# Attention products of the sample tokens with the values, issued between the dense matmuls of the next unit

## The reference

```python
D_MODEL, SEQ, DEC_SEQ, PAST_LEN = 2048, 256, 64, 256
N_HEADS, HEAD_DIM = 16, 128

h = _rms_norm(x, g_mix)
z = h @ w_in                      # GLU a, b | q | k | v | indexer | gates
...
s = jnp.einsum('qhd,qkhd->qhk', q, kg) * HEAD_DIM ** -0.5
s = jnp.where(valid[:, None, :], s, -jnp.inf)
p = jax.nn.softmax(s, axis=-1)
o = jnp.einsum('qhk,qkhd->qhd', p.astype(v.dtype), vg)
...
m = jax.nn.sigmoid(ga) * c + jax.nn.sigmoid(gb) * (o @ w_attn_out)
x = x + m @ w_out
h = _rms_norm(x, g_ffn)
x = x + (jax.nn.silu(h @ w_gate) * (h @ w_up)) @ w_down
```

## Time and profile before

| | us |
|---|---|
| median of 3 runs | 2058.59 |
| lowest and highest run | 2056.78, 2058.63 |
| span of the profiled execution | 2055.5 |

### The profile page before, as it was taken

How to read it: one execution, slowest core, us unless ns; L and a number is a source line. 1 busy time by engine, 2 the same in 40 slices (tenths; PEclk the granted TensorE clock), 3 DMA queues, 4 the chain that set the end, 5 groups by cost and what they waited for, 6 DMA issues and landing times.

```text
span 2055.5 us, 37840 instructions
## 1 busy us (share of the span) xinstructions
PE 2036.4 (99%) x13897; PEld 2018.5 (98%) x13897; DVE 1116.9 (54%) x1658; ACT 810.4 (39%) x1133; POOL 44.6 (2%) x55
## 2 busy tenths in 40 slices
PE   9999999999999999999999999999999999999997
PEld 8999999999999999999999999999999999999997
DVE  6865777778876343344546444445444333344454
ACT  5633344444446333333334333333333232333343
POOL 2200000000020000000000000000000000000000
PEclk9999999999999999999999999999999999999999
DMA  7445566666655545444445454454454454454443
GB/s 199 123 144 155 154 165 163 155 168 161 164 138 159 155 150 153 143 143 143 143 153 162 140 159 149 137 163 147 139 163 148 139 162 144 143 155 141 143 133 112
DMA packets 362094, 308.84 MB, mean 150 GB/s; under 512 B 74271, under 2 KB 359543, under 8 KB 362048
## 3 DMA queue, kind: packets, MB, share of 16 engines
q1 hardware_dynamic: 360832, 305.32, 50.4%
q0 software_dynamic: 1184, 2.90, 0.5%
q10 hardware_dynamic: 32, 0.01, 0.0%
HBM read 299.98 MB, written 8.19 MB: 150 GB/s over the span
## 4 chain that ended last, share of the span: by engine, by line
PE 97%; DMA 1%; DVE 1%; SPq 0%; ACT 0%; issue 0%; DVEq 0%
PE M L589 26%; PE M L591 26%; PE M L590 26%; PE T L590 5%; PE T L591 5%; PE T L589 5%; DMA x_tok<-in_x_prompt 1%; PE T L768 0%; PE S L746 0%; DVE c_all L1660 0%; DMA v_tok<-out_v_s 0%; PE S L744 0%; PE S L899 0%; PE S L745 0%; PE S L657 0%; PE T L772 0%
## 5 line engine op out<-in xcount | busy, mean ns | idle before, releaser
L1303 DVE TENSOR_TENSOR w_lo<-w_raw,w_hi 128x1024 fp32r<-128x1024 f32 (+1 forms) x556 | 669.2, 1219 | 544.7 <-ACT w_hi L942 531.9
L942 ACT ACTIVATE w_hi<-w_raw 128x1024 fp32r<-128x1024 f32 (+1 forms) x556 | 574.4, 1051 | 581.6 <-PE M L591 398.6
L589 PE MATMUL M<-h_hi,w_hi 128*128 128x320 f32 x1792 | 560.0, 312 | 0.9 <-DVE w_lo L1303 0.9
L591 PE MATMUL M<-h_hi,w_lo 128*128 128x320 f32 x1792 | 553.7, 309 | 0.0
L590 PE MATMUL M<-h_lo,w_hi 128*128 128x320 f32 x1792 | 553.6, 309 | 0.0
L589 PE MATMUL M<-o_hi,w_hi 128*128 128x320 f32 x1664 | 513.5, 309 | 0.0
L591 PE MATMUL M<-o_hi,w_lo 128*128 128x320 f32 x1664 | 513.1, 308 | 0.0
L590 PE MATMUL M<-o_lo,w_hi 128*128 128x320 f32 x1664 | 513.1, 308 | 0.0
L589 PEld LDWEIGHTS M<-h_hi,w_hi 128*128 128x128 f32 x1792 | 336.5, 188 | 3.0 <-issue 2.4
L590 PEld LDWEIGHTS M<-h_lo,w_hi 128*128 128x128 f32 x1792 | 336.5, 188 | 0.5
L591 PEld LDWEIGHTS M<-h_hi,w_lo 128*128 128x128 f32 x1792 | 336.3, 188 | 0.0
(11 more groups left out here) (303 smaller groups left out, 1267.9 us busy)
## 6 DMA issues: line engine op xcount, KB each, us to landing
w_raw<-in_w_in SPq DMA_DIRECT2D x208, 512.0 KB, 3.9
w_raw<-in_w_gate SPq DMA_DIRECT2D x88, 512.0 KB, 4.5
w_raw<-in_w_up SPq DMA_DIRECT2D x88, 512.0 KB, 4.4
w_raw<-in_w_down SPq DMA_DIRECT2D x88, 512.0 KB, 3.4
w_raw<-in_w_attn_out SPq DMA_DIRECT2D x32, 512.0 KB, 5.1
w_raw<-in_w_out SPq DMA_DIRECT2D x32, 512.0 KB, 3.5
w_raw<-in_w_conv_out SPq DMA_DIRECT2D x16, 512.0 KB, 3.5
x_tok<-in_x_prompt SPq DMA_DIRECT2D x4, 512.0 KB, 9.0
```

The source lines that it names most:

```text
L589: mm(out, w_hi[:, s, wc:wc + m], x_hi, start=start, stop=False)
L591: done = mm(out, w_lo[:, s, wc:wc + m], x_hi, start=False, stop=stop)
L942: act_fn(w_hi[:, s, 0:n], w_raw[:, s, 0:n], ACT.Copy).then_inc(hi_ready, 1)
L1303: v.tensor_tensor(w_lo[:, s, 0:n], w_raw[:, s, 0:n], w_hi[:, s, 0:n].bitcast(f32), ALU.subtract)\
```

## The change

`attend` issues only the two prompt products of an out step. The three sample products become a list of three calls, `sample_out(h)`. The next unit gets them as `between` and issues one of them behind each of its first three slices of block 0, that is behind its 3rd, 6th and 9th dense matmul. pv_done is still signalled by the third. In W_HEAD out 0 goes into unit 7 and out 1 into unit 9; for the last pair out 0 goes into unit 6 of the first merge iteration and out 1 into unit 8. The waits stay where they were, ahead of the prompt products. No other engine's program changes.

```diff
+            BETWEEN_AT = ((0, 0), (0, 1), (0, 2))
+
+            def unit(ph, i, u, k0, first, last, banks, hi, lo, n=NU, free=None, part=None, between=()):
...
                         done = mm(out, w_lo[:, s, wc:wc + m], x_hi, start=False, stop=stop)
+                        if (b, kk) in BETWEEN_AT[:len(between)]:
+                            between[BETWEEN_AT.index((b, kk))]()
...
                     mm(out[:, P:TP], v_tok[:, 1, hc], pT[:, TP:PP], start=False, stop=True)
-                    mm(out[:, TP:T], cv_tok[:, 0, hc], pT_past[:, h * TS:(h + 1) * TS], start=True, stop=False)
-                    mm(out[:, TP:T], cv_tok[:, 1, hc], pT_past[:, P + h * TS:P + (h + 1) * TS], start=False, stop=False)
-                    mm(out[:, TP:T], v_tok[:, 2, hc], pT[:, PP + h * TS:PP + (h + 1) * TS], start=False, stop=True)\
-                        .then_inc(pv_done, 1)
+
+            def sample_out(h):
+
+                hc = slice(h * P, (h + 1) * P)
+                out = T0[:, 3 * TS + TP:3 * TS + T]
+                return (lambda: mm(out, cv_tok[:, 0, hc], pT_past[:, h * TS:(h + 1) * TS], start=True, stop=False),
+                        lambda: mm(out, cv_tok[:, 1, hc], pT_past[:, P + h * TS:P + (h + 1) * TS],
+                                   start=False, stop=False),
+                        lambda: mm(out, v_tok[:, 2, hc], pT[:, PP + h * TS:PP + (h + 1) * TS],
+                                   start=False, stop=True).then_inc(pv_done, 1))
+
+            def between_of(step):
+                return sample_out(int(step[-1])) if step in ("out 0", "out 1") else ()
...
+                def inside(u):
+                    return between_of(HEAD_STEPS[u - 1]) if 1 <= u <= len(HEAD_STEPS) else ()
+                head_units(i, extra, inside)
...
+            def last_pair_inside(u):
+                return between_of(HEAD_STEPS[u]) if 6 <= u < 9 else ()
+
+            merge_units(0, last_pair_and_norm, last_pair_inside)
```

More of the change, by code:

```diff
@@ L568, in _ @@
             TILES = ((2, T - P), (0, 0), (1, P))
-            def unit(ph, i, u, k0, first, last, banks, hi, lo, n=NU, free=None, part=None):
+            BETWEEN_AT = ((0, 0), (0, 1), (0, 2))
+            def unit(ph, i, u, k0, first, last, banks, hi, lo, n=NU, free=None, part=None, between=()):
                 s = u % 4
@@ L769, in attend, with head_units @@
                     mm(out[:, P:TP], v_tok[:, 1, hc], pT[:, TP:PP], start=False, stop=True)
-                    mm(out[:, TP:T], cv_tok[:, 0, hc], pT_past[:, h * TS:(h + 1) * TS], start=True, stop=False)
-                    mm(out[:, TP:T], cv_tok[:, 1, hc], pT_past[:, P + h * TS:P + (h + 1) * TS], start=False, stop=False)
-                    mm(out[:, TP:T], v_tok[:, 2, hc], pT[:, PP + h * TS:PP + (h + 1) * TS], start=False, stop=True)\
-                        .then_inc(pv_done, 1)
+            def sample_out(h):
[8 more added lines that the diff above has]
+                return sample_out(int(step[-1])) if step in ("out 0", "out 1") else ()
             pe.sem_inc(pv_done, 1)
-            def head_units(i, extra):
+            def head_units(i, extra, inside=None):
                 for u in range(12):
@@ L786, in head_units @@
                         free = (act_evac, lambda b: at(ACT_EV, W_HEAD, i, b + 1))
-                    unit(W_HEAD, i, u, KU * (u % 4), u % 4 == 0, u % 4 == 3, SET[g % 2], h_hi, h_lo, free=free)
+                    unit(W_HEAD, i, u, KU * (u % 4), u % 4 == 0, u % 4 == 3, SET[g % 2], h_hi, h_lo, free=free,
+                         between=() if inside is None else inside(u))
                     extra(u)
@@ L813, in extra, with merge_units @@
                         attend(i - 1, HEAD_STEPS[u])
-                head_units(i, extra)
-            def merge_units(i, extra=None):
+                def inside(u):
+                    return between_of(HEAD_STEPS[u - 1]) if 1 <= u <= len(HEAD_STEPS) else ()
+                head_units(i, extra, inside)
+            def merge_units(i, extra=None, inside=None):
                 for u in range(14):
@@ L832, in merge_units @@
                     last = u in (3, 7, 11, 13)
-                    unit(W_MERGE, i, u, KU * (u % 4), u % 4 == 0, last, SET[g % 2], hi, lo, free=free, part=part)
+                    unit(W_MERGE, i, u, KU * (u % 4), u % 4 == 0, last, SET[g % 2], hi, lo, free=free, part=part,
+                         between=() if inside is None else inside(u))
                     if extra is not None:
@@ L851, in last_pair_and_norm @@
                     attend(PAIRS - 1, HEAD_STEPS[u + 1])
-            merge_units(0, last_pair_and_norm)
+            def last_pair_inside(u):
+                return between_of(HEAD_STEPS[u]) if 6 <= u < 9 else ()
+            merge_units(0, last_pair_and_norm, last_pair_inside)
             with pe.Fori(1, W_MERGE.loops) as i:
```

## The result

The changed kernel takes 2066.79 us (median of 5 runs, 2065.87 to 2067.07) against 2058.59 us of the kernel before (5 runs, 2056.78 to 2060.42). The ratio is 1.0041, with a 95% interval of 1.0029 to 1.0053: 0.4% slower, 8.2 us. The forecast was 2066.5.

The account below looks back on a forecast made before the run. TensorE, busy for 99% of the span, was taken to bound the kernel. 0 for the order, 7.6 for seven pairs and 0.3 for the last gave 2058.6 + 7.9 = 2066.5 us, range 2063.5 to 2068.5, chance 0.74.

Parts of the forecast that it names:

- The order costs TensorE nothing: On TensorE, the three moved products of an out step still take 0.67 us, so reordering costs 0.
- The signal 1.32 us late, whole at v_blocks: pv_done comes nine dense matmuls later; VectorE has no idle time from o_lo, so v_blocks ends 1.32 us later.
- 1.08 us for each pair: TensorE waits for v_blocks at the next pair's unit 0, 1.08 us in each of seven pairs, 7.6 us.
- 0.3 us in the last pair: In the first merge iteration, TensorE waits for unit 9's late w_lo: 0.3 us, bounds 0 and 0.5.
- The sum: Whole kernel: 0 for the order, 7.6 for seven pairs and 0.3 for the last make 7.9 us slower.
- hidden loads: Rival on TensorE: weight loads hidden gain 5.6 us, the stall stays at 7.9; 2060.9 us, chance 0.10.
- the wait that VectorE absorbs: Rival: VectorE catches up between o_lo and v_blocks, no stall and no gain; 2058.6 to 2059 us, chance 0.08.
- the faster case: Rival: TensorE's loads hidden and no stall at v_blocks, 5.6 us gained; 2053.0 us, chance 0.05.
- the dearer one: Rival: dense-short borders cost extra or each pair has a second wait, +10 to +12, 2069 to 2071 us; chance 0.03.

Follow-up runs that it names:

- out 0 alone: Of the change only out 0's three sample products moved between dense matmuls, out 1 left as in the kernel before: 2057.42 us, ratio 0.9998 to the kernel before.
- double_columns: The kernel before, with 128 columns in place of 64 streamed in each of the three sample products: 2058.52 us, ratio 0.9999.
- half_weights: The kernel before, with 64 instead of 128 weight columns loaded for each of the three sample products: 2058.35 us, ratio 1.0002.
- v_blocks_early: The changed kernel, with VectorE's two v_blocks transposes of a pair queued earlier and the late signal kept: 2059.41 us, ratio 1.0008 to the kernel before.

## Why the prediction was right, step by step

- **The order costs TensorE nothing.** Right: 0.66 against 0.67 us for three products, 48.03 us a pair with the wait taken away, 48.04 with out 0 alone. The prediction's sentence that a sum of this kind doesn't depend on order is too general: which load stands behind which matmul does depend on it, and the sum stays the same here because all these loads take the same 0.112 us. The reason, that the loads set the pace and that each is made one matmul ahead and not two, is borne out by double_columns and by the loads of the changed kernel: the second pass's load (290.96 with two loads, the dense one behind them at 291.22) and the dense load each take their 0.11 us beside a short pass. The rule of the Trainium skill (TensorE: Matmul & The Clock Gate, "Step-by-step: what each phase is for") that loads are pulled ahead of matmuls in flight agrees with these rows for one matmul ahead; read generously, for more than one, it would have given 5.6 us, and the trace shows none of them.
- **The signal 1.32 us late, whole at v_blocks.** Right. VectorE's 8.73 us from o_lo to v_blocks are the same in both kernels.
- **1.08 us for each pair.** The mechanism and the place were right, the size was 0.06 to 0.09 too large: 1.02 by the rows of the first border, 0.99 by the length of a pair. The row that I priced it by, a wait for w_lo, has the matmul 0.15 us after the recorded end of VectorE's instruction; here it is 302.80 - 302.74 = 0.06 us. The bounds (0.92 to 1.15) held it. 7.0 instead of 7.6 us.
- **0.3 us in the last pair.** The wait came at the size forecast, but the total doesn't show it. Ahead of unit 9 of the first merge iteration:

```profile
637.29 1.22 DVE L1322 TENSOR_TENSOR w_lo<-w_raw,w_hi 128x1024 fp32r<-128x1024 f32 x1
...
638.25 0.31 PE L592 MATMUL M<-o_hi,w_lo 128*128 128x320 f32 x1
638.65 0.39 PE L590 MATMUL M<-o_hi,w_hi 128*128 128x320 f32 x1
638.87 0.30 PE L591 MATMUL M<-o_lo,w_hi 128*128 128x320 f32 x1
```

  The second matmul stands 0.62 us behind 638.25, not 0.29: 0.33 us lost, as forecast. The prediction had left out that this iteration holds another wait of TensorE, for the transfer of v_tok. It was 1.4 us in the kernel before, as its list of waits shows, and is 1.1 in the changed one:

```profile
PE T L768 <- DMA v_tok<-out_v_s: 1.4, 1, 1.4
```

  In this pair of traces the two cancel. Why the transfer's wait fell is open: in the ten traces it takes from 0.7 to 1.5 us, and 0.9 and 0.7 in double_columns and half_weights, which move no product. So it may be scatter, and the cancelling luck.
- **The sum.** 7.0 us are located, the medians differ by 8.2. In the two profiled executions the spans differ by 8.7 us: 7.0 in the pairs, and 1.7 ahead of the first pair, where the programs are the same. The first v_blocks of all, before and after:

```profile
250.67 0.52 DVE L1619 STREAM_TRANSPOSE v_blocks<-M 128x320 f32<-128x320 f32 x1 [1.65 <-PE M L591]
```

```profile
252.36 0.52 DVE L1638 STREAM_TRANSPOSE v_blocks<-M 128x320 f32<-128x320 f32 x1 [1.64 <-PE M L592]
```

  In the ten traces of this study that point lies anywhere from 250.3 to 253.7 us, without order by the kind of change (250.28 with out 0 alone, 253.69 in half_weights), so I take it as scatter of the start. That the medians' remaining 1.2 us is the same scatter is likely, not shown: the 7.0 us lie inside the interval of the difference (6.0 to 10.9 us). The forecast's total of 7.9 was thus met in part by luck: its terms hold 0.9 more than the traces locate, and the medians 1.2 more.

Of the four rivals, hidden loads fell by v_blocks_early, the wait that VectorE absorbs fell by the seven rows, the faster case with both, and of the dearer one (borders, a second wait in each pair) the changed kernel shows nothing.

No kernel here is faster than the one before by more than its interval. The short products already run at the rate of their loads, and with the wait removed the two orders take the same time within the interval (ratio 0.9999 to 1.0017).

## What to carry to other kernels

Moving short matmuls between long ones hid nothing here, where each weight load is made only one matmul ahead: the time is the sum, over all matmuls, of the longer of a matmul's streaming and the load behind it. With all loads of one length that sum has no order; with loads of different lengths or widths the order can matter. Before interleaving, look at what hangs on the last of the moved products, and follow that signal through the queues of the other engines to the next thing that the bounding engine needs from them; here the slack at that point was 0.3 us, three queues away, and the signal was delayed by 1.3. An idle time ahead of a wait (1.90 us of VectorE here) is not slack if the queue behind it is full up to a deadline.

## What the runs showed of the hardware

- A weight load of 128 columns in 4-byte elements takes 0.112 us of the engine's time, one of 64 columns 0.058 at most; streaming takes 0.84 ns a column in each pass of an fp32 product. Doubling the columns of the short products from 64 to 128 was free (ratio 0.9999, 0.67 us in both).
- Not expected: at a change of the weights' width between successive matmuls, 128 columns to 64, the load isn't made ahead. It started 0.24 us later than a load of 128 columns does in the same place; with the border back to 128 columns that took away all that the smaller load saved (ratio 1.0002).
- Between the recorded end of a VectorE instruction and the start of the matmul that waited for it there were 0.06 us for a transpose and 0.15 for a subtraction; the price of a wait from one kind of row is good to about 0.1 us.
